# State update laid into the next inverse, and part of the new values' decay on ScalarE, in a gated delta rule recurrence

## The chip, the core and the metric

The kernel runs on one NeuronCore of a Trainium2 chip. The metric is the device time of one execution in microseconds (us). Engines are named as the profile names them: PE is TensorE, DVE is VectorE, ACT is ScalarE, POOL is GpSimd, SP is SyncE, which here only issues DMAs. PE writes its products to PSUM, which has eight banks of 128 x 512 f32; the other engines carry them to SBUF.

## The reference, cut to what matters

Two blocks of a network run one after the other: a mixer with a gated delta rule and a pooling branch, then feed-forward layers, a short convolution and latent attention. Only the gated delta rule is touched. It works on 8 heads in two directions, over 512 tokens (256 of context, then 256 with queries). The reference uses chunks of 64 tokens; the kernel uses chunks of 128, which gives the same values:

```python
a_mat = jnp.where(strict, jnp.einsum('bhncd,bhnsd->bhncs', kb, k) * decay, 0.0)
sol = lax.linalg.triangular_solve(eye + a_mat, rhs, ...)        # rhs = [v*beta, kb*exp(g)]
qk = jnp.einsum('bhncd,bhnsd->bhncs', q, k) * decay
k_tail = k * jnp.exp(g_last[..., None] - g)[..., None]
def step(state, inp):
    v_new = u_i - jnp.einsum('bhcd,bhdv->bhcv', w_i, state)
    o_i = (jnp.einsum('bhcd,bhdv->bhcv', q_i, state)
           + jnp.einsum('bhcs,bhsv->bhcv', qk_i, v_new))
    state = state * jnp.exp(gl_i)[..., None, None] + jnp.einsum('bhcd,bhcv->bhdv', k_i, v_new)
    return state, o_i
```

## The kernel before

**Rounds.** `ROUNDS` (L1167) holds 8 rounds: four chunks (`step_` 0 to 3) times two groups of four heads. A round has two sides, one batch of four heads each: forward (FWD, banks 0 to 2) and backward (BWD, banks 3 to 5). The state that a round reads was made two rounds before, by the same heads. Chunks 0 and 1 are context; in chunks 2 and 3 the outputs of the queries are made as well; chunk 3 makes no state.

**One round.** In the order of PE's program: the inverse of the lower triangular matrix (`inverse`, L1271) by four levels of doubling in 64 x 64 halves, each a left product (L1294) into bank b0+2, an ACT copy (L1468), a right product (L1311) into bank b0+1, a DVE addition (L1621) and a DVE transpose (L1623); the transposes of `a` (L1302) lie in level 1; rounds with queries have the products of keys and queries (L1317) in level 2; then the steps to 64 and 128 tokens (L1326, L1337, L1342, L1351, L1360). After that the keys times the state (L1376, from chunk 1 on), the running sums of the decays for the next round (`sums`, L1248), four parts of the modulation (`some_mods` "state"), the new values (L1386), the Gram matrix of the next round (`gram`, L1256), the outputs (L1398, L1400), two modulation parts ("out"), the new state (L1409), the transposed keys of the next round (`key_rows`, L1268) and six modulation parts ("gram").

**Around PE.** DVE copies the end of the inverse to `xt` (L1643), forms `rhs` (L1651; L1656 in chunk 0), half of the decay argument (L1608, L1609), the new values with their decayed tail (L1662), the masked Gram matrix (L1579), the outputs (L1671, L1674), the state (L1680, L1684) and, last, `first_blocks` (L1582) for both sides, whose result `ac` (L1594) the first left product of the next round waits for. ACT makes the decay (`decay`: four Relu, L1427, and one Exp, L1431), for rounds with queries also a second decay for `pt` (L1441, L1445), and copies. POOL makes masks and products in SBUF: L1522, L1530, L1542, L1548, L1552, L1558.

**Modulation.** In the rounds PE also multiplies 96 parts of 512 KB of another weight matrix (`mod_part`, L577, products at L587), 12 a round, at places fixed by `MOD_SLOTS` (L1181). They come through a ring of six buffers: SP asks for part p once part p-6 is used. The next stage starts on ACT only after the copy of the last group (L613), and the weights of that stage are asked for after the last part.

**Order.** Every engine runs its program in order; all waits between engines are semaphores written out by hand, so an instruction that waits holds all behind it on its engine.

Of the kernel before, what the change touches and what calls it, by code (L numbers as in the profile page):

```python
# [206 lines left out]
def two_block_kernel(nc, stream, modstream, tokens, ctx2, conds, cols_in, consts_in, rope_tab, count_in, out):  # L207
# [47 lines left out]
    for d in (FWD, BWD):  # L255
        for room, names in (("inner", ("ac", "atc")), ("outer", ("xc", "xtc"))):
# [4 lines left out]
            .rearrange("p l (j c) -> p l j c", j=4)  # L261
        W[d]["t1h"] = W[d]["t1"][:, 0:2, :].rearrange("p a b -> p (a b)").rearrange("p (j c) -> p j c", j=4)
# [907 lines left out]
    a_dec, a_pt, a_qd, a_kt, a_at, a_t1, a_vn = (sem(f"a_{n}") for n in ("dec", "pt", "qd", "kt", "at", "t1", "vn"))  # L1170
# [3 lines left out]
    a_pair, a_xt, a_relu, a_ptr = (sem(f"a_{n}") for n in ("pair", "xt", "relu", "ptr"))  # L1174
    xt_clear = sem("xt_clear")
    d_relu = sem("d_relu")
# [4 lines left out]
    MOD_SLOTS = {"state": 4, "out": 2, "gram": 6}  # L1181
# [39 lines left out]
    def packed(b, rows=slice(0, P), width=PAIR):  # L1221

        return bank[b][rows, 0:4 * width].rearrange("p (j c) -> p j c", j=4)
# [5 lines left out]
    def pe_recur(pe):  # L1229
# [14 lines left out]
        def sums(r):  # L1244
            for n, d, t, hs, b0, gc in per_batch(r):
                if r:
                    pe.wait_ge(d_xf, n - 1)
                four(lambda j: nc.tensor.matmul(  # L1248
                    b4(b0)[:, j], gb_tok[:, t, gc][:, j:j + 1].to_broadcast([P, P]), C(Const.INCL[d]),
                    start=True, stop=True), g_cb)  # L1250

        def gram(r):
            for n, d, t, hs, b0, gc in per_batch(r):
                if r:
                    pe.wait_ge(d_rhs, n - 1)
                four(lambda j: nc.tensor.matmul(  # L1256
                    b4(b0 + 1)[:, j], kT[:, hs, tok(t)][:, j], kT[:, hs, tok(t)][:, j],
                    start=True, stop=True), g_gram)

        def key_rows(r):  # L1260
            step_ = ROUNDS[r][0]
            for n, d, t, hs, b0, gc in per_batch(r):
                pe.wait_ge(a_dec, n + 1)
                if step_ >= 2:
                    pe.wait_ge(a_qd, n - X_BATCH0 + 1)
                    pe.wait_ge(a_pt, n - X_BATCH0 + 1)
                if step_ < 3:
                    four(lambda j: nc.tensor.transpose(b4(b0)[:, j], kT[:, hs, tok(t)][:, j],  # L1268
                                                       C(Const.IDENT)), g_kt)

        def inverse(r):  # L1271
# [3 lines left out]
            for li in range(1, 5):  # L1275
                for n, d, t, hs, b0, gc in batches:
                    w = W[d]
                    if li == 1:
                        pe.wait_ge(d_at, n + 1)
                        if r:  # L1280
                            pe.wait_ge(d_vdec, n - 1)
                            if ROUNDS[r - 1][0] < 3:
                                pe.wait_ge(d_state, n - 1)
                            if ROUNDS[r - 1][0] >= 2:
                                pe.wait_ge(d_o, n - 1 - X_BATCH0)
                    elif li == 2:
                        pe.wait_ge(p_at, nth(2, r, 0, d))
                    elif li == 4:
                        pe.wait_ge(p_at, nth(2, r, 1, d))
                    pe.wait_ge(d_xm, nth(5, r, li - 1, d))  # L1290
                    at_li = w["ac"] if li == 1 else w["atl"][:, li % 2]
                    for j in range(4):
                        for i in range(2):
                            last = nc.tensor.matmul(packed(b0 + 2, half(i))[:, j], at_li[half(i), j], w["xc"][half(i), j],  # L1294
                                                    start=True, stop=True)
                    last.then_inc(g_p1, 1)
                if li == 1:
                    for n, d, t, hs, b0, gc in batches:
                        pe.wait_ge(d_a, n + 1)
                        if step_ < 3:  # L1300
                            pe.wait_ge(a_kt, n + 1)
                        four(lambda j: nc.tensor.transpose(b4(b0)[:, j], W[d]["a"][:, j], C(Const.IDENT)), g_at)  # L1302
                for n, d, t, hs, b0, gc in batches:
                    w = W[d]
                    pe.wait_ge(a_t1, nth(6, r, li - 1, d))
                    pe.wait_ge(d_xt, nth(5, r, li - 1, d))
                    if li == 1:
                        pe.wait_ge(d_gm, n + 1)
                    for j in range(4):
                        for i in range(2):  # L1310
                            last = nc.tensor.matmul(packed(b0 + 1, half(i))[:, j], w["xtc"][half(i), j],  # L1311
                                                    w["t1h"][half(i), j], start=True, stop=True)
                    last.then_inc(g_p2, 1)
                if li == 2 and with_x:
# [54 lines left out]
        for r, (step_, hg) in enumerate(ROUNDS):  # L1369
# [8 lines left out]
            if r + 1 < len(ROUNDS):  # L1378
                sums(r + 1)
# [8 lines left out]
            if r + 1 < len(ROUNDS):  # L1388
                gram(r + 1)
# [1205 lines left out]
```

## Time and profile before

| | us |
|---|---|
| median of 3 runs (2462.14 to 2470.65) | 2464.55 |
| the profiled execution | 2467.92 |
| its span in the profile | 2466.1 |
| recurrence, first sums to the first product of the next stage | 323.10 to 658.18 |
| PE busy in the span | 2328.3 (94%) |
| DVE, ACT, POOL busy | 966.4, 791.2, 1025.9 |
| mean granted clock of PE | 0.958 |

Below, a round is counted from the first record of L1360 of the round before to its own first L1360; the inner stretches of the first group of rows are cut there. The rows that the prediction rests on stand in a section below.

### The profile page before, as it was taken

How to read it: one execution, taken by the hardware profiler on the slowest of the kernel's cores; microseconds unless marked ns; L12 is line 12 of the kernel's file. 1: busy time of each engine (PE TensorE's matmuls, PEld its weight loads, DVE VectorE, ACT ScalarE, POOL GpSimd, SP SyncE). 2: the span in 40 equal slices, each digit the busy share in tenths (PEclk: the TensorE clock that was granted, in tenths of full speed). 3: DMA queues.
4: the chain of work that ended last, by engine and by line, in shares of the span. 5: the costliest groups of instructions: out<-in, count | busy, mean ns of one | idle time of the engine just before them, and what ended most of it. 6: DMA issues, size and time to landing. Idle time of an engine off the chain costs nothing.

```text
span 2466.1 us, 36821 instructions
## 1 busy us (share of the span) xinstructions
PE 2328.3 (94%) x14268; PEld 1852.7 (75%) x14268; DVE 966.4 (39%) x1631; ACT 791.2 (32%) x1247; POOL 1025.9 (42%) x473
## 2 busy tenths in 40 slices
PE   6998788898889999999999999999999999898999
PEld 2787667676667888887887888887888887547999
DVE  4459656656363121124455122124112114755212
ACT  2443423334223222223223222223222222424444
POOL 1445612233252444443443444443444443304888
PEclk8999878999898999999999999999999999989999
DMA  6334414525561433332532533332433332202656
GB/s 244 94 104 128 162 54 154 206 105 183 181 232 63 162 94 94 94 94 86 171 94 77 171 94 95 94 94 77 160 96 95 94 94 77 74 0 81 189 179 184
DMA packets 82682, 297.38 MB, mean 121 GB/s; under 512 B 9072, under 2 KB 11504, under 8 KB 82288
## 3 DMA queue, kind: packets, MB, share of 16 engines
q1 hardware_dynamic: 82400, 295.03, 37.1%
q8 instruction: 107, 1.75, 0.3%
q10 hardware_dynamic: 144, 0.34, 0.0%
q14 instruction: 31, 0.25, 0.0%
HBM read 294.28 MB, written 1.05 MB: 120 GB/s over the span
## 4 chain that ended last, share of the span: by engine, by line
PE 77%; issue 11%; DVE 6%; POOL 4%; ACT 1%; DMA 1%; POOLq 0%; SPq 0%; DVEq 0%; ACTq 0%
PE bank L547 21%; PE bank L544 21%; PE bank L543 21%; POOL w_lo L519 4%; PE bank L587 2%; PE bank L1294 1%; PE bank L1311 1%; PE bank L1248 1%; PE bank L918 1%; DVE gdn_inner L1588 1%; PE bank L2147 1%; DVE nt L751 1%; PE bank L2148 1%; PE bank L1376 1%; PE bank L1256 1%
## 5 line engine op out<-in xcount | busy, mean ns | idle before, releaser
L519 POOL TENSOR_TENSOR w_lo<-w_raw,w_hi 128x1024 fp32r<-128x1024 f32 x383 | 934.7, 2444 | 1181.2 <-ACT w_hi L771 1180.9
L543 PE MATMUL bank<-n_hi,w_lo 128*128 128x512 f32 (+1 forms) x2216 | 793.3, 358 | 30.9 <-POOL w_lo L519 16.3
L547 PE MATMUL bank<-n_lo,w_hi 128*128 128x512 f32 (+1 forms) x2216 | 792.1, 357 | 0.6 <-DVE n_lo L695 0.3
L544 PE MATMUL bank<-n_hi,w_hi 128*128 128x512 f32 (+1 forms) x2216 | 791.3, 357 | 0.0
L771 ACT CAST w_hi<-w_raw 128x1024 fp32r<-128x1024 f32 x383 | 401.1, 1049 | 776.1 <-PE bank L547 766.3
L543 PEld LDWEIGHTS bank<-n_hi,w_lo 128*128 128x128 f32 x2216 | 423.4, 191 | 116.3 <-issue 44.6
L544 PEld LDWEIGHTS bank<-n_hi,w_hi 128*128 128x128 f32 x2216 | 423.6, 191 | 64.5
L547 PEld LDWEIGHTS bank<-n_lo,w_hi 128*128 128x128 f32 x2216 | 422.6, 191 | 64.6 <-DVE n_lo L695 2.5
L1955 DVE TENSOR_TENSOR prod<-silu,bank 128x512 f32<-128x512 f32 (+1 forms) x88 | 54.6, 622 | 728.9 <-PE bank L547 721.4
L544 PE MATMUL bank<-g_hi,w_hi 128*128 128x512 f32 (+1 forms) x768 | 284.1, 370 | 0.0
L547 PE MATMUL bank<-g_lo,w_hi 128*128 128x512 f32 (+1 forms) x768 | 284.1, 370 | 0.0
L543 PE MATMUL bank<-g_hi,w_lo 128*128 128x512 f32 (+1 forms) x768 | 282.3, 368 | 1.1 <-DVE g_lo L1946 1.1
L1917 DVE SCALAR_TENSOR_TENSOR h<-bank,gates,h 128x256 f32<-128x256 f32 x136 | 60.7, 481 | 301.2 <-PE bank L547 301.1
L543 PEld LDWEIGHTS bank<-g_hi,w_lo 128*128 128x128 f32 x768 | 144.4, 188 | 29.1 <-DVE g_lo L1946 1.5
L544 PEld LDWEIGHTS bank<-g_hi,w_hi 128*128 128x128 f32 x768 | 144.3, 188 | 27.4
L547 PEld LDWEIGHTS bank<-g_lo,w_hi 128*128 128x128 f32 x768 | 144.1, 188 | 26.1
L1903 ACT ACTIVATE silu<-bank 128x512 f32<-128x512 f32 (+1 forms) x88 | 47.7, 544 | 286.1 <-PE bank L547 286.0
L1035 DVE SCALAR_TENSOR_TENSOR conv<-bank,cols,conv 128x508 f32<-128x508 f32 (+3 forms) x96 | 63.0, 659 | 60.7 <-ACT conv L975 58.1
L1946 DVE TENSOR_TENSOR g_lo<-prod,g_hi 128x512 fp32r<-128x512 f32 (+1 forms) x88 | 82.8, 943 | 1.8 <-ACT g_hi L1893 1.5
L751 DVE TENSOR_TENSOR nt<-h 128x512 f32<-128x512 f32 (+1 forms) x77 | 78.6, 1021 | 2.6
L587 PE MATMUL bank<-mod_raw,cond 128*32 128x512 f32 x256 | 54.9, 694 | 22.0 <-DMA mod_raw<-in_modstream 18.3
L756 DVE TENSOR_TENSOR sq_acc<-sq_acc,nt 128x512 f32<-128x512 f32 (+1 forms) x66 | 62.0, 939 | 2.3
(317 smaller groups left out, 2036.3 us busy)
## 6 DMA issues: line engine op xcount, KB each, us to landing
w_raw<-in_stream SPq DMA_DIRECT2D x383, 512.0 KB, 3.6
mod_raw<-in_modstream SPq DMA_DIRECT2D x64, 512.0 KB, 4.6
late<-in_modstream SPq DMA_DIRECT2D x56, 512.0 KB, 4.7
w_raw<-in_modstream SPq DMA_DIRECT2D x48, 512.0 KB, 6.2
h<-in_tokens SPq DMA_DIRECT2D x1, 2048.0 KB, 10.8
consts<-in_consts SPq DMA_DIRECT2D x1, 1152.0 KB, 9.9
h<-in_ctx SPq DMA_DIRECT2D x1, 1024.0 KB, 8.7
out<-h SPq DMA_DIRECT2D x8, 128.0 KB, 3.6
```

The costliest lines, as they stand in the source:

```text
L519: nc.gpsimd.tensor_tensor(w_lo[:, slot, :], w_raw[:, slot, :], w_hi[:, slot, :].bitcast(F32), ALU.subtract).then_inc(w_lo_ready, 1)
L543: nc.tensor.matmul(out_ap, wl, hi, start=start, stop=False)
L544: nc.tensor.matmul(out_ap, wh, hi, start=False, stop=False)
L547: return nc.tensor.matmul(out_ap, wh, lo, start=False, stop=stop)
L587: last = nc.tensor.matmul(bank[MOD_BANK][32 * j:32 * j + 32, :], cond[:, which, k, :], room[:, jj * 512:(jj + 1) * 512], start=(k == 0), s ...
L751: square = nc.vector.tensor_tensor(nt[:, k % 2, s_], h[:, k, s_], h[:, k, s_], ALU.mult)
L756: ins = nc.vector.tensor_tensor(sq_acc[:, s_], sq_acc[:, s_], nt[:, k % 2, s_], ALU.add)
L771: nc.scalar.copy(w_hi[:, c % RING, :], w_raw[:, c % RING, :]).then_inc(w_hi_ready, 1)
L1035: ins = nc.vector.scalar_tensor_tensor(acc[:, :, to], src[:, :, of], col(Cols.CONV + ci * CONV + j), acc[:, :, to], ALU.mult, ALU.add)
L1917: last = nc.vector.scalar_tensor_tensor(h[:, d, s_], bank[g % BANKS][:, s_], gates[:, gate, d, c:c + 1], h[:, d, s_], ALU.mult, ALU.add)
L1946: nc.vector.tensor_tensor(g_lo[:, f, 0:w], prod[:, f % 2, 0:w], g_hi[:, f, 0:w].bitcast(F32), ALU.subtract).then_inc(hid_lo, 1)
L1955: nc.vector.tensor_tensor(prod[:, f % 2, 0:w], silu[:, f % 2, 0:w], bank[g % BANKS][:, 0:w], ALU.mult).then_inc(groups_read, 2)
```

## The change

It reorders the recurrence and moves some of its work between engines; the same 96 modulation parts and the same products are made.

- The new state of round r-1 (`new_state`) is made inside the inverse of round r: after the first left product of the forward side if round r-1 had no queries, after level 1 if it was of chunk 2. DVE's `state_sum` follows behind levels 1 to 3.
- The transposed keys (`key_rows`) are made in their own round, behind level 1, instead of one round ahead; the transposes of `a` go from level 1 to behind level 2, the products of keys and queries from level 2 to level 3, the keys times the state from behind the inverse to between left and right product of level 4. `rhs` is formed right behind level 4.
- After the inverse PE runs, side by side, Gram matrix, sums, new values of FWD, then the same of BWD.
- Left products write to the upper half of bank b0+1, not to bank b0+2.
- In the rounds without queries (chunks 0 and 1) the decayed tail of the new values is made by ACT (four Identity with a scale, semaphore `a_vdec`), not by DVE. In chunk 3 it is not made at all.
- ACT makes the decay argument of both sides, with Abs in the place of Relu; DVE's L1608 and L1609 are gone. `pt` is now masked `dec` (by POOL); ACT's second decay (L1441, L1445) is gone.
- DVE's `first_blocks` no longer holds the product L1600; it is `whole`, behind the additions of level 1. Its waits at the joint: Gram matrix of both sides before `first_blocks` of FWD.
- POOL: the mask of level 2 (`at2`) is a product of its own right behind `atc`; `atl` holds levels 3 and 4; beta masks are made into `a` one round ahead.
- Modulation parts: "first" 2 (in level 1), "half" 3 (behind L1326), "last" 3 (behind L1351), "key" 4 (end of the round).

```diff
-    MOD_SLOTS = {"state": 4, "out": 2, "gram": 6}
+    MOD_SLOTS = {"first": 2, "half": 3, "last": 3, "key": 4}
...
+        def gram(r, side):
+            n, d, t, hs, b0, gc = per_batch(r)[side]
+            if r:
+                pe.wait_ge(a_t1, nth(6, r - 1, 5, d))
+                pe.wait_ge(d_half, n - 1)
...
+        def new_state(r):
+            for n, d, t, hs, b0, gc in per_batch(r):
+                if ROUNDS[r][0] < 2:
+                    pe.wait_ge(a_vdec, n + 1)
+                else:
+                    pe.wait_ge(d_vdec, n - X_BATCH0 + 1)
+                    pe.wait_ge(d_o, n - X_BATCH0 + 1)
+                four(lambda j: nc.tensor.matmul(b4(b0 + 2)[:, j], W[d]["ktok"][:, j], W[d]["rhs"][:, j],
+                                                start=True, stop=True), g_st)
...
+            late_state = r and ROUNDS[r - 1][0] == 2
+            left(r, 1, FWD)
+            if r and ROUNDS[r - 1][0] < 2:
+                new_state(r - 1)
+            right(r, 1, FWD)
+            some_mods(r, "first")
+            left(r, 1, BWD)
+            right(r, 1, BWD)
+            if late_state:
+                new_state(r - 1)
+            if step_ < 3:
+                key_rows(r)
+            for d in (FWD, BWD):
+                left(r, 2, d)
+            for d in (FWD, BWD):
+                right(r, 2, d)
...
+            for d in (FWD, BWD):
+                left(r, 4, d)
+            for d in (FWD, BWD):
+                keys_state(r, d)
+            for d in (FWD, BWD):
+                right(r, 4, d)
...
                 last.then_inc(g_p1, 1)
+            some_mods(r, "half")
...
                 last.then_inc(g_p1, 1)
+            some_mods(r, "last")
...
             inverse(r)
...
+            for d in (FWD, BWD):
+                if r + 1 < len(ROUNDS):
+                    gram(r + 1, d)
+                    sums(r + 1, d)
+                new_values(r, d)
+            if step_ >= 2:
...
+            some_mods(r, "key")
...
+            for n, d, t, hs, b0, gc in batches:
+                if r + 1 < len(ROUNDS):
+                    decay(r + 1, d)
+                if not with_x:
+                    act.wait_ge(g_vn, n + 1)
+                    for j in range(4):
+                        last = nc.scalar.activation(W[d]["rhs"][:, j], b4(b0 + 2)[:, j], ACT.Identity,
+                                                    scale=e_tail[:, t, gc.start + j:gc.start + j + 1])
+                    last.then_inc(a_vdec, 1)
...
+            more = r + 1 < len(ROUNDS)
+            if more:
+                masked_gram(r + 1, FWD)
+            values_decay(r, FWD)
+            if more:
+                masked_gram(r + 1, BWD)
+                first_blocks(r + 1, FWD)
+            values_decay(r, BWD)
+            if more:
+                first_blocks(r + 1, BWD)
+            turned_groups(r, "key")
```

## Rows read from the trace of the kernel before

**Rows 1.** Windows: stretch, length, busy PE PEld DVE ACT POOL (records), clock, DMA, GB/s.
```profile
323.10:351.86 28.76, 22.18 (x401) 20.15 (x401) 16.89 (x38) 9.55 (x25) 4.09 (x4) 0.80 0.01 2
351.86:388.98 37.12, 33.73 (x497) 25.78 (x497) 23.11 (x46) 11.45 (x31) 8.30 (x8) 0.87 0.47 171
388.98:426.29 37.31, 34.39 (x500) 25.90 (x500) 23.30 (x48) 12.00 (x32) 8.30 (x8) 0.86 0.48 171
426.29:463.91 37.62, 34.02 (x516) 26.75 (x516) 23.69 (x60) 12.01 (x32) 8.12 (x8) 0.91 0.47 169
463.91:504.26 40.35, 36.40 (x529) 28.77 (x529) 24.63 (x60) 16.21 (x44) 13.00 (x12) 0.92 0.44 158
504.26:548.71 44.45, 39.92 (x565) 32.57 (x565) 26.16 (x64) 17.02 (x45) 13.09 (x12) 0.92 0.40 143
548.71:591.99 43.28, 38.90 (x557) 31.68 (x557) 26.23 (x64) 16.53 (x44) 13.05 (x12) 0.92 0.43 148
591.99:631.27 39.28, 35.28 (x540) 27.12 (x540) 23.92 (x56) 16.43 (x44) 13.09 (x12) 0.96 0.46 162
631.27:658.18 26.91, 20.11 (x132) 12.63 (x133) 9.36 (x22) 5.82 (x12) 4.97 (x4) 0.75 0.49 173
```
**Rows 2.** The chain that ended last, over one joint: start, length, what.
```profile
390.60 3.78 PE bank L1248 x16
394.38 2.49 PE bank L587 x16
396.87 1.98 PE bank L1386 x16
398.86 1.79 PE bank L1256 x16
400.64 1.00 PE bank L587 x8
401.64 2.00 PE bank L1409 x16
...
408.47 1.41 DVE gdn_inner L1588
...
411.51 0.68 PE bank L1294 x16
...
417.49 0.43 DVE gdn_outer L1621
...
422.49 0.43 DVE gdn_outer L1621
```
**Rows 3.** Timeline, PE: start, length, engine, line, operation, tiles, forms, records.
```profile
592.98 2.05 PE L1376 MATMUL bank<-state,kT 128*128 128x128 f32 x16
366.12 1.04 PE L1268 MATMUL bank<-consts,kT 128*128 128x128 f32 x8
```
**Rows 4.** Timeline, DVE, ACT and POOL, same columns; idle time before in brackets.
```profile
392.71 1.14 ACT L1427 ACTIVATE gdn_dec<-bank,neg_cum 128x128 f32<-128x128 f32 x4 [1.84 <-PE bank L1248]
393.89 0.63 ACT L1431 ACTIVATE gdn_dec<-gdn_dec 128x512 f32<-128x512 f32 x1
408.21 1.37 POOL L1542 TENSOR_TENSOR gdn_dec<-gdn_inner,consts 128x512 f32<-128x512 f32 x1 [3.30 <-DVE gdn_a L1600]
440.30 2.16 DVE L1684 SCALAR_TENSOR_TENSOR state<-state,e_tot,bank 128x128 f32<-128x128 f32 x8 [1.32 <-PE bank L1409]
```
**Rows 5.** Two stretches behind the inverse, columns as in rows 1.
```profile
388.98:395.00 6.02, 6.00 (x36) 5.10 (x40) 3.47 (x5) 3.62 (x10) 2.22 (x2) 0.50 0.01 3
591.99:595.00 3.01, 3.01 (x34) 2.94 (x35) 1.60 (x5) 1.85 (x5) 1.80 (x2) 1.00 0.00 0
```
**Rows 6.** Timeline: ACT changing its table, and PE around the end of the recurrence.
```profile
301.71 1.28 ACT L1014 ACT_TABLE_LOAD   x1
645.43 1.07 PE L587 MATMUL bank<-w_raw,cond 128*32 128x512 f32 x8
651.25 1.57 PE L587 MATMUL bank<-w_raw,cond 128*32 128x512 f32 x4 [0.19 <-DMA w_raw<-in_modstream]
```

More of the change, by code:

```diff
@@ new lines, in left @@
+        def left(r, li, side):
+            n, d, t, hs, b0, gc = per_batch(r)[side]
+            w = W[d]
+            if li == 1:
+                pe.wait_ge(d_at, n + 1)
+                pe.wait_ge(d_gm, n + 1)
+            elif li == 2:
+                pe.wait_ge(p_at, nth(2, r, 0, d))
+            elif li == 3:
+                pe.wait_ge(p_at, nth(2, r, 1, d))
+            pe.wait_ge(d_xm, nth(5, r, li - 1, d))
+            at_li = w["ac"] if li == 1 else w["at2"] if li == 2 else w["atl"][:, li - 3]
+            for j in range(4):
+                for i in range(2):
+                    last = nc.tensor.matmul(upper(b0 + 1, half(i))[:, j], at_li[half(i), j], w["xc"][half(i), j],
+                                            start=True, stop=True)
+            last.then_inc(g_p1, 1)
@@ new lines, in right @@
+        def right(r, li, side):
+            n, d, t, hs, b0, gc = per_batch(r)[side]
+            w = W[d]
+            pe.wait_ge(a_t1, nth(6, r, li - 1, d))
+            pe.wait_ge(d_xt, nth(5, r, li - 1, d))
+            for j in range(4):
+                for i in range(2):
+                    last = nc.tensor.matmul(packed(b0 + 1, half(i))[:, j], w["xtc"][half(i), j],
+                                            w["t1h"][half(i), j], start=True, stop=True)
+            last.then_inc(g_p2, 1)
@@ L1274, in inverse @@
             with_x = step_ >= 2
-            for li in range(1, 5):
-                for n, d, t, hs, b0, gc in batches:
[L1277 to L1314, printed above, removed]
-                    for n, d, t, hs, b0, gc in batches:
-                        pe.wait_ge(a_at, n + 1)
-                        four(lambda j: nc.tensor.matmul(b4(b0)[:, j], kT[:, hs, tok(t)][:, j],
-                                                        qT[:, hs, tok(t)][:, j], start=True, stop=True), g_qk)
@@ L1483, in act_recur @@
                 act.wait_ge(g_p1, nth(6, r, 5, d))
-                nc.scalar.copy(W[d]["t1h"][hi], packed(b0 + 2, hi)).then_inc(a_t1, 1)
+                nc.scalar.copy(W[d]["t1h"][hi], upper(b0 + 1, hi)).then_inc(a_t1, 1)
+            mods_copied(r, "last")
             for n, d, t, hs, b0, gc in batches:
@@ L1616, in dve_recur @@
             with_x = step_ >= 2
-            for li in range(1, 5):
+            late = r and ROUNDS[r - 1][0] == 2
+            if r and ROUNDS[r - 1][0] >= 2:
+                outputs(r - 1)
+            for d in (FWD, BWD):
+                add_level(r, 1, d)
+                whole(r, d)
+            turned_groups(r, "first")
+            if r and not late:
+                state_sum(r - 1, FWD)
+            for d in (FWD, BWD):
+                add_level(r, 2, d)
+            if r:
+                state_sum(r - 1, FWD if late else BWD)
```

450 lines of the change are left out of this document (225 added, 225 removed).

## The prediction

> **What bounds the kernel now.** I read first the windows over the recurrence [rows 1]. It is 335.1 us of the 2466.1 us span, and only it and the hand-over behind it are touched. PE is busy for about nine tenths of each round (33.7 of 37.1 us, 39.9 of 44.5 us), so PE's program, in order, is the bound; two things make its round long. First, the clock: in rounds 1 to 7 it is 0.86 to 0.96. A stretch that is at half clock for half its length has a mean of 0.75 and could be a quarter shorter, so the time that a full clock could save is at most (1 - clock) times the length: 4.8, 5.2, 3.4, 3.2, 3.6, 3.5 and 1.6 us, 25.3 us in all. Second, the joint between rounds. The chain of waits shows it [rows 2]: behind the inverse PE runs sums, modulation, new values, Gram matrix, modulation and state one after the other (390.60 to 403.6); then the chain leaves PE and goes through DVE's two `first_blocks`, until the left product at 411.51. In those 8 us PE has only modulation and one side's left product. The clock view of the stretches says when the clock falls: behind the run of 32 x 32 and 64 x 64 products it was 0.50 for 6 us in one round and stayed 1.00 in another [rows 5].
>
> **The sum, part by part.** I lay round 2 (37.31 us before, 388.98 to 426.29) out anew from S, the first L1360, at full clock. Durations: eight products of 128 x 128 take 1.79 to 2.05 us (0.9 a side) [rows 2, 3]; a transposition of both sides 1.0 [rows 3]; two modulation parts 1.0 [rows 2]; one level of doubling 2.5 (417.49 to 422.49 are two) [rows 2].
>
> 1. Joint. L1360 1.1 (estimate: its share at full clock), then Gram, sums, new values, F and B: 6 x 0.9 = 5.4, at 6.5. "key" four parts 2.0, at 8.5. Who is late next? ACT's decay of F waits for the sums of F (2.9): 1.14 + 0.63 [rows 4] gives 4.8; the decayed tail of F four small activations, about the 1.14 of L1427, 6.0; decay of B 7.8; tail of B 9.0. DVE: Gram B 5.5, `first_blocks` F without L1600 about 3.0, `ac` at 8.1, B `ac` at 11.5. Both come before PE wants them, within half a microsecond for F; so they are covered, and each microsecond by which ACT or DVE is later costs one.
> 2. Level 1. Left F 0.6, new state 2.0 (its wait for ACT's tail of B, 9.0, is met at 9.1; queued behind it are right F and all of the inverse), right F 0.6, two parts 1.0, left B 0.6, gap for the ACT copy 0.5, right B 0.6: at 14.4. Keys 1.0: 15.4.
> 3. Levels 2 and 3 with the transposes of `a`: 2.5 + 1.0 + 2.5, at 21.4. DVE has two additions with transposes, `whole` 0.65 and 1.1 of L1684 a level, which fits in 2.5 + 1.0. A POOL product of SBUF beside L1684 did not lengthen it (2.16 for eight [rows 4]).
> 4. Level 4 with the keys times the state: 2.5 + 2.0 less the 0.5 gap that these fill, at 25.4.
> 5. Last steps: from the addition at 422.49 to L1360 at 426.29 are 3.8, that is 3.2 from the end of the right product of B. Now 3 + 3 parts lie in them, 3.0, and nothing hides these: 31.6.
>
> So 31.6 against 37.3. PE's work is the same; what goes is the stretch of `first_blocks` in which it had little to do, and half clock behind the inverse. DVE's L1608, L1609 and L1662 and ACT's L1441 and L1445 go too; the walk above has them left out already, and they are worth nothing beyond that. No modulation part should wait for its data: a part of "key" reuses a buffer that was free with "half" or "last", at least 6 us before.
>
> A collision: the chain has a `first_blocks` product of 1.41 us instead of 0.42, beside a POOL product of 1.37 [rows 2, 4]. `at2` on POOL starts as DVE does L1592 and L1594. Bounds a side: 0, or the whole of `at2`, 0.7 (estimate: half the elements of L1542 and its 1.37). I take 0 on the path, since `ac` of F has 0.4 to spare and `ac` of B 2, and keep 0.3 a round, 2 us, for the range. The Trainium skill (SBUF — State Buffer, "SBUF: two separate sides") says that a DVE operation with two SBUF inputs and a GpSimd operation exclude each other for the whole instruction. By that rule every round would pay the upper bound, and the sum would be 2 us less gain; the trace agrees with it in the one pair of rows.
>
> The other rounds, by the same walk: round 1 (no keys times state) 29.9; round 3 31.6; round 4 (keys times queries, 1.5 net of a hidden gap) 33.2. Rounds 5 to 7 have the outputs in the joint. The new values of B are decayed by DVE behind `first_blocks` F (9.6), ACT's copy follows (10.3), so the outputs of B run 10.4 to 12.2, "key" ends at 14.1 and all is 5.6 later than in round 2; with the new state behind level 1: round 5 39.5, round 6 (no keys) 38.5, round 7 (no state either) 36.7.
>
> | | before [rows 1] | new | gain |
> |---|---|---|---|
> | 1 | 37.1 | 29.9 | 7.2 |
> | 2, 3 | 37.3, 37.6 | 31.6 each | 5.7, 6.0 |
> | 4 | 40.4 | 33.2 | 7.2 |
> | 5 | 44.5 | 39.5 | 5.0 |
> | 6 | 43.3 | 38.5 | 4.8 |
> | 7 | 39.3 | 36.7 | 2.6 |
>
> That is 38.5. The first stretch (28.8) gets the keys and eight modulation parts before its L1360, and its `first_blocks` B is 1 us shorter; its clock is 0.80, so I add 2.8: -2.8. The last stretch: today outputs end 14.2 behind S (645.43), the last part is used only at 652.8, since two buffers came free late (PE waits for DMA at 651.25 [rows 6]), and the next stage starts 5.4 later (658.18). Anew: xt and new values F at 2.9, B at 3.8, outputs to 7.5, with latencies 8.1; four parts, data long there, 2.0; then the same 5.4 and 0.7 for DVE's squares beside POOL's products: 16.2 against 26.9, 10.7 gained. Sum: 38.5 - 2.8 + 10.7 = 46.4 us.
>
> The clock: the walk took it as full. The new order puts 512-column products into the run behind which it fell, and takes away PE's idle stretch, but a PE that is now the bound pays every half-clock microsecond. Bounds: 0, and the 25.3 us of today. I take a quarter, 6.5, nearer to the stretch that stayed at 1.00 [rows 5]. So 2467.9 (the profiled execution) - 46.4 + 6.5 = 2428.0; the median of the runs lies 3.4 below that execution: **2424.5**.
>
> **The rivals.**
> - *The clock falls as it did.* The joint's gain comes, the clock's doesn't: 46.4 - 25.3 = 21, 2443.5. For it: the long middle of the inverse is unchanged small products. Against: they ran at 1.00 before, and the fall came behind the smallest.
> - *ACT is late at the new wait.* If Abs and Exp need different tables, each batch of decays pays 2 x 1.28 [rows 6], 5.1 a round before the tail of B; `new_state` waits 4.8 in rounds 1 to 4, the outputs of B 2.6 in 5 to 7: 27 us back, 2451.5. Against: Relu and Exp have stood side by side with no load between them [rows 4]. The Trainium skill (ScalarE: Activation LUTs, "Table sets: the hidden batching unit") says that abs is in every set; by it there is no load, and by its 2.7 us a switch the loss would be twice mine. No row here shows Abs.
> - *The time was covered anyway*: the joint's waits come back as DVE's chain (`first_blocks` 3 us later than in the walk in every round, from new latencies). 7 rounds x 3 to 5 us off a gain of 40 leave 5 to 19; at the small end 2459.5, no change.
> - *Slower: PE stays at half clock.* The work of a round is now one chain of short products with ACT and DVE between; if the granted clock is that of the last stretch, 0.75 [rows 1], a round of 40 us pays 10, seven pay 70: 46.4 - 70 = -23.6, 2488. It decides from a mean clock under 0.83 in the rounds (46.4 over 280 us); the lowest of them today is 0.86, so it must get worse than in any round shown.
>
> **How the numbers follow.** Forecast 0.62; clock as before 0.17; ACT late 0.07; covered anyway 0.07; slower 0.07. The forecast's own range is 2412 (clock full, all of the 46 and some) to 2437. To leave out no more than 2 in 10 the range goes up to the clock rival: 2411 to 2446. A measurement of this kernel can tell about 0.3%, 7.4 us, from no change. Faster by more than that are the first three and 0.02 of the fourth, 0.88; the rest of the fourth is no change, 0.05; slower 0.07.
>
> **What would show it.** Rounds of 30 to 33 us between first L1360s in 1 to 4 and 37 to 40 in 5 to 7; granted clock 0.95 or more in them; PE's idle before the first left product under 1 us; no DMA wait at L587; no ACT table load in the rounds; L1588's twin for B at 0.42. Wrong if PE waits for `a_vdec` before the new state, if `ac` of F comes more than 1 us behind the "key" parts, if outputs of B start over 11 us behind S, or if the last stretch stays over 20 us.

## The result

| | before | after |
|---|---|---|
| median of 4 runs, us | 2464.91 (2462.14 to 2470.65) | 2430.30 (2425.90 to 2433.95) |
| profiled execution, its span | 2467.92, 2466.1 | 2428.83, 2427.0 |
| ratio of the times, 95% interval | | 0.9856, 0.9831 to 0.9881 |
| first stretch: first sums to first L1360 (before), L1421 (after) | 28.76 | 31.35 |
| rounds 1 to 7, sum | 279.4 | 249.1 |
| last stretch: from there to the first product of the next stage | 26.91 | 15.59 |

The times are 1.4% shorter, where 2424.5 in a range of 2411 to 2446 was forecast. L1421 is the line that was L1360. To be set against the rows of before [rows 1], the windows of the kernel after, cut at its first L1421 of each inverse (stretch, length, busy PE PEld DVE ACT POOL with records, granted clock, DMA share, GB/s):

```profile
323.10:355.82 32.72, 27.02 (x434) 19.64 (x433) 17.33 (x40) 11.87 (x33) 8.16 (x8) 0.86 0.21 68
355.82:387.77 31.95, 30.04 (x503) 22.10 (x501) 18.52 (x42) 15.38 (x45) 8.16 (x8) 1.00 0.59 215
387.77:420.08 32.31, 31.08 (x516) 23.71 (x513) 20.17 (x50) 12.82 (x38) 8.16 (x8) 1.00 0.52 181
420.08:452.96 32.88, 31.74 (x518) 24.04 (x517) 21.04 (x56) 15.96 (x46) 8.16 (x8) 1.00 0.56 194
452.96:487.78 34.82, 33.58 (x535) 25.99 (x533) 22.62 (x58) 15.68 (x46) 13.26 (x12) 1.00 0.50 184
487.78:529.61 41.83, 37.63 (x567) 29.51 (x565) 24.95 (x60) 15.60 (x41) 13.27 (x12) 1.00 0.46 165
529.61:568.81 39.20, 35.83 (x556) 28.41 (x553) 25.20 (x62) 12.03 (x32) 13.27 (x12) 1.00 0.40 145
568.81:604.91 36.10, 34.35 (x542) 26.78 (x541) 21.69 (x52) 15.17 (x40) 11.28 (x10) 1.00 0.51 181
604.91:620.50 15.59, 9.13 (x86) 7.18 (x85) 7.61 (x12) 4.42 (x9) 5.40 (x4) 0.95 0.53 198
```

Two things are to be seen. The clock column is 1.00 in all seven rounds (before 0.86 to 0.96). And a round of 32.31 us has 31.08 of PE busy, so 1.2 us of idle where there were 2.9. Over rounds 1 to 7, with the same products, PE is busy for 234.3 us instead of 252.6 and idle for 14.8 instead of 26.8: of the 30.3 us by which the rounds are shorter, 18.3 are busy time, the same products at a higher clock, and 12.0 are waiting that is gone. In this execution the first sums begin at 324.47, 1.37 later than before, so the first stretch is 31.35 long. From first sums to the next stage the recurrence takes 296.0 instead of 335.1, 39.1 less; the span is 39.1 shorter. Outside the recurrence nothing was gained on balance: 1.4 us more ahead of it, 1.4 less behind (1806.5 against 1807.9).

What PE still waits for in rounds 1 to 7 (line, who ends the wait, us in all, times, longest). L1309 is a right product, L1447 the outputs, L1385 the first products of the step to 64, L588 a modulation part:

```profile
PE bank L1309 <- ACT gdn_t L1479: 4.7, 10, 0.5
PE bank L1447 <- DVE gdn_rhs L1688: 3.5, 2, 1.8
PE bank L1385 <- DVE gdn_outer L1654: 2.4, 7, 0.3
PE bank L588 <- ACT mod_row L614: 1.6, 2, 0.8
```

The 15.1 us that PE waited for DVE's `ac` before (L1594) have no line any more. The joint of round 2, in which this was won; S, its first L1421, is at 387.77. The columns are start, length, engine, line; `ac` is written by L1639, and L1582 is POOL's `at2`:

```profile
392.61 0.69 DVE L1624 SCALAR_TENSOR_TENSOR gdn_a<-bank,gdn_a 128x512 f32<-128x512 f32 x1 [1.99 <-PE bank L1261]
393.21 0.84 DVE L1633 TENSOR_TENSOR gdn_inner<-gdn_a,gdn_dec 64x256 f32<-64x256 f32 x2
...
395.22 0.95 DVE L1639 TENSOR_TENSOR gdn_inner<-gdn_inner,consts 128x256 f32<-128x256 f32 x1
...
398.44 0.95 DVE L1639 TENSOR_TENSOR gdn_inner<-gdn_inner,consts 128x256 f32<-128x256 f32 x1
...
395.08 0.82 POOL L1582 TENSOR_TENSOR gdn_t<-gdn_inner,consts 128x256 f32<-128x256 f32 x1 [17.89 <-DVE gdn_inner L1636]
...
395.18 1.12 ACT L1536 ACTIVATE gdn_rhs<-bank,e_tail 128x128 f32<-128x128 f32 x4
```

`ac` F is ready at 396.17, 8.4 behind S, as the four parts of "key" end; ACT's tail of B at 396.30 (8.5); `ac` B at 399.39 (11.6), a microsecond before its left product (400.43).

### The profile page after: what moved, and what is told of

It is laid out like the page before. It is cut to its first block, busy times and chain, and to the rows that moved or that the text cites. A ratio compares the mean times of both kernels' runs of the same rounds, so it can differ in the third digit from the quotient of the medians.

```text
span 2427.0 us, 36815 instructions
## 1 busy us (share of the span) xinstructions
PE 2302.1 (95%) x14268; PEld 1826.4 (75%) x14268; DVE 948.4 (39%) x1603; ACT 793.1 (33%) x1271; POOL 1027.2 (42%) x473
## 4 chain that ended last, share of the span: by engine, by line
issue 52%; PE 23%; POOL 20%; DVE 4%; ACT 1%; POOLq 1%; DVEq 0%; ACTq 0%
POOL w_lo L520 20%; PE bank L544 3%; PE bank L545 3%; PE bank L548 3%; PE bank L588 2%; PE bank L1298 1%; PE bank L1309 1%; PE bank L919 1%; PE bank L2218 1%; PE bank L1261 1%; PE bank L2219 1%; PE bank L2259 1%; PE bank L1281 0%; PE bank L1252 0%; PE bank L2236 0%
## 5 line engine op out<-in xcount | busy, mean ns | idle before, releaser
L1582 POOL TENSOR_TENSOR gdn_t<-gdn_inner,consts 128x256 f32<-128x256 f32 x16 | 13.1, 817 | 174.6 <-DVE gdn_inner L1636 174.6
L588 PE MATMUL bank<-mod_raw,cond 128*32 128x512 f32 x256 | 62.2, 685 | 18.8 <-DMA mod_raw<-in_modstream 18.8
```

The lines of the kernel that those rows point to most:

```text
L588: last = nc.tensor.matmul(bank[MOD_BANK][32 * j:32 * j + 32, :], cond[:, which, k, :], room[:, jj * 512:(jj + 1) * 512], start=(k == 0), s ...
```

## The experiments

Where the order is the same and the clock full, round lengths repeat to 0.1 us from one profiled execution to another (rounds 1 to 4 of after, a_vdecb), so each run is read by its rounds, and the total only confirms. Each run has one profile; where the clock falls in a run is known from that one alone. "Falls" counts the stretches of 1 us windows with the clock under 0.95, behind an inverse (eight of them) and elsewhere in rounds 1 to 7.

| run | median us | ratio to before | rounds 1 to 7 | last stretch | falls behind the inverse / elsewhere |
|---|---|---|---|---|---|
| before | 2464.9 | | 279.4 | 26.9 | 7 / 6 |
| after | 2430.3 | 0.9856 | 249.1 | 15.6 | 0 / 0 |
| b_slots | 2462.8 | 0.9994 (0.9984 to 1.0003) | 281.9 | 19.0 | 0 / 7 |
| a_slots | 2483.1 | 1.0081 (1.0064 to 1.0098) | 295.3 | 20.3 | 6 / 0 |
| a_mid | 2454.8 | 0.9953 (0.9937 to 0.9968) | 271.0 | 17.6 | 8 / 0 |
| a_mid2 | 2443.9 | 0.9916 (0.9898 to 0.9935) | 255.9 | 18.2 | 5 / 0 |
| a_joint | 2445.9 | 0.9926 (0.9910 to 0.9943) | 265.2 | 15.6 | 0 / 2 |
| a_state | 2429.1 | 0.9862 (0.9846 to 0.9879) | 251.1 | 15.6 | 0 / 0 |
| a_dvestate | 2451.4 | 0.9939 (0.9918 to 0.9959) | 274.9 | 15.6 | 0 / 4 |
| a_both | 2454.9 | 0.9952 (0.9936 to 0.9967) | 276.7 | 15.6 | 0 / 5 |
| a_vdec | 2426.9 | 0.9843 (0.9816 to 0.9869) | 249.3 | 15.6 | 0 / 0 |
| a_vdecb | 2423.6 | 0.9832 (0.9805 to 0.9860) | 245.1 | 15.6 | 0 / 0 |
| a_at2 | 2429.9 | 0.9852 (0.9823 to 0.9882) | 247.5 | 15.6 | 0 / 0 |
| a_best | 2420.4 | 0.9813 (0.9800 to 0.9827) | 244.8 | 11.8 | 0 / 0 |

The ratio is to the kernel before as it ran beside each run. The code cuts below are shortened; what stands in them as a comment tells what is left out.

My theory was that the gain has two parts, a shorter joint (`ac` comes in time) and the clock (by where the modulation parts stand). The rivals: all is clock; or all is order.

The falls elsewhere go with waits of PE in the joint. All 24 of them (in five of the kernels) begin during, or within 2.3 us behind, a wait of 1.5 to 3.6 us, 20 times the wait for `ac`. Such a wait did not always bring one: a_joint has four waits for `ac` of up to 1.9 us in rounds 1 to 4 and no fall there.

**b_slots: the parts moved, in the kernel before.**

```diff
-    MOD_SLOTS = {"state": 4, "out": 2, "gram": 6}
+    MOD_SLOTS = {"half": 3, "last": 3, "state": 2, "gram": 4}
```

> The kernel before with the modulation parts alone moved: three behind the 32 x 32 products, three behind the last left products of 64 x 64, two in "state", four in "gram", none in "out". My theory: two separate gains. The clock follows the place of the wide products, so it is 0.97 or more in rounds 1 to 7 (before 0.86 to 0.96); but the joint keeps its order, and with six parts fewer in it PE idles about 3 us more a round before the first left product. A round with no queries is 36 to 37.5 us (before 37.1 to 37.6), the last stretch some 5 us shorter: total 2452 to 2462. Rival (all is clock): rounds 1 to 4 fall to 32 to 35 us as in the changed kernel, total about 2435. Rival (place of the parts does nothing to the clock): clock stays 0.86 to 0.96, total 2465 or more.

Measured 2462.8, no change, and 0.8 us above what I expected. The clock of the rounds is 0.92 to 0.96, not the 0.97 that I expected: the falls behind the inverse are gone, but seven others stand in the joints. PE's wait for `ac` over rounds 1 to 7 in the kernel before, then round 2 of this one as a window and the same wait:

```profile
PE bank L1294 <- DVE gdn_inner L1594: 15.1, 6, 3.5
```
```profile
394.68:431.16 36.48, 30.97 (x504) 23.46 (x500) 23.27 (x48) 11.36 (x31) 8.35 (x8) 0.95 0.47 165
```
```profile
PE bank L1294 <- DVE gdn_inner L1596: 25.2, 12, 3.6
```

The clock rose from 0.86 to 0.95 and PE's busy time fell by 3.4 us [rows 1], but the round is only 0.8 shorter. PE waits for `ac` 10 us longer in the seven rounds: the joint ran at DVE's pace, and what PE saved it idled. "All is clock" falls here, since moving the parts alone gave nothing. In all, the rounds are 2.5 longer and the first stretch, which gets the six parts of "half" and "last", 4.4; the last stretch is 7.9 shorter. So most of the 11.3 us that the changed kernel gains in the last stretch can be had by the place of the parts alone.

**a_slots, a_mid, a_mid2: the parts moved, in the kernel after.**

```diff
-    MOD_SLOTS = {"first": 2, "half": 3, "last": 3, "key": 4}
+    MOD_SLOTS = {"first": 5, "half": 0, "last": 0, "key": 7}        # a_slots
+    MOD_SLOTS = {"first": 2, "mid": 6, "key": 4}                    # a_mid: "mid" ahead of left product 3
```

> The changed kernel with its modulation parts put together around the joint: five in "first", seven in "key", none in "half" and "last". My theory: the clock falls behind the smallest products as in the kernel before, mean 0.88 to 0.96 in rounds 1 to 7, which costs 12 to 25 us in the rounds, and the last stretch grows by 2 to 6 us for parts that come late: total 2444 to 2458. Rival (the clock is held up by the absence of PE's idle stretch, not by the parts' place): clock 1.00, rounds as in the changed kernel within 0.5 us, total 2430 to 2436.

Measured 2483.1, beyond both. Twelve parts close together ("key", then "first") need their data faster than they come: over the recurrence PE waited 14.2 us for DMA (12.3 for `w_raw`, 1.9 for `mod_raw`), and 8.1 for the half copies L1738 that stand behind `rhs` in DVE's program. So this run can't price the clock, which fell behind six of eight inverses. It led to a_mid, which spreads the data as before.

> The changed kernel with the six modulation parts of "half" and "last" put together into the middle of the inverse, between the transposes of `a` and level 3, so that the data come as evenly as before and the joint keeps its four parts. My theory: parts beside the smallest products do two things, they keep the clock up behind the inverse and they hide `rhs` and ACT's last copies. So the clock falls to one half for 4 us or more behind the inverse in most rounds (2 us or more each), PE waits 1.4 us for the half copies and up to 1 us for copies of ACT: rounds 1 to 7 longer by 3 to 5 us each, total 2451 to 2464. Rival (the clock fell only because PE idled in the joint): clock 1.00 in rounds 1 to 7, the waits alone remain, 1.4 to 2.5 us a round, total 2440 to 2448.

Measured 2454.8, in the range expected: rounds 21.9 longer in all (2.3 to 4.7 each, where I said 3 to 5), and the clock falls behind every inverse. Round 3's beginning, in windows of 1 us:

```profile
422.00:423.00 1.00, 0.96 (x63) 0.85 (x56) 1.00 (x5) 0.65 (x3) 0.00 (x0) 1.00 0.09 37
423.00:424.00 1.00, 0.19 (x13) 0.08 (x6) 1.00 (x5) 0.64 (x3) 0.00 (x0) 1.00 0.08 20
424.00:425.00 1.00, 0.46 (x9) 0.46 (x11) 0.75 (x3) 0.00 (x0) 0.00 (x0) 1.00 0.00 0
425.00:426.00 1.00, 0.87 (x15) 0.72 (x13) 0.00 (x0) 0.72 (x3) 0.00 (x0) 0.70 0.00 0
426.00:427.00 1.00, 1.00 (x16) 1.00 (x14) 0.18 (x1) 0.96 (x4) 0.00 (x0) 0.50 0.02 8
```

and its wait for the half copies over the rounds:

```profile
PE bank L1411 <- DVE gdn_outer L1737: 8.1, 6, 1.4
```

PE waits 1.35 us for the half copies, until 424.54, and about 0.9 us later, at 425.4, is at half clock. So the idle, not the lack of wide products, could be the cause; a_mid2 takes that wait away:

```diff
             for n, d, t, hs, b0, gc in batches:
+                src, dst = first_pair(d)
+                dve.wait_ge(g_p2, nth(5, r, 4, d))         # and the half copy itself
+            for n, d, t, hs, b0, gc in batches:
                 w = W[d]
                 dve.wait_ge(p_rhs, n + 1)
...
-                src, dst = first_pair(d)
-                dve.wait_ge(g_p2, nth(5, r, 4, d))         # and the half copy itself
```

> As the run with the six parts in the middle of the inverse, and DVE makes the two half copies ahead of `rhs`, so that PE's 1.4 us of idle before the last left products goes. It tells apart what lets the clock fall behind the inverse. Theory 1 (idle of PE): with the wait gone the clock stays 1.00 in rounds 2 to 7, which are shorter by 1.4 for the wait and by 1.5 to 3 for the clock: total 2430 to 2438. Theory 2 (small products without wide ones beside them, idle or not): the falls behind the inverse stay in every round at 0.57 for 4 to 8 us, rounds are shorter by 1.4 at most, total 2445 to 2449. I think the first the likelier, since in the trace of that run the fall begins 1 us behind the idle stretch.

Measured 2443.9, between the two. The rounds are 15.1 us shorter, 8.1 of it the wait; the falls went from eight to five. My likelier theory was too simple. In two rounds whose last microseconds are alike, the clock fell once and once not:

```profile
425.00:426.00 1.00, 0.75 (x40) 0.67 (x40) 0.67 (x3) 0.43 (x2) 0.00 (x0) 1.00 0.17 66
```

That window stands 1.7 us ahead of S of round 3 (427.66), behind which the clock was 0.50; the one in the same place of round 4 had 0.76 busy and kept 1.00. The lack of wide products is enough in some rounds. That idle ahead of the smallest products makes the fall surer is a hint, eight falls against five with one profile of each. With three parts at each of the two places (after, b_slots) it fell behind none of sixteen. Why it falls in one of two like rounds stays open.

**a_joint: the products of the joint in sequence.**

```diff
             for d in (FWD, BWD):
-                if r + 1 < len(ROUNDS):
+                if more:
+                    sums(r + 1, d)
+            for d in (FWD, BWD):
+                new_values(r, d)
+            for d in (FWD, BWD):
+                if more:
                     gram(r + 1, d)
-                    sums(r + 1, d)
-                new_values(r, d)
```

> The changed kernel with the joint in sequence on PE as before: sums of both sides, new values of both, Gram matrix of both. Everything else stays. My theory: the masked Gram matrix of the forward side starts 3.6 us later but the decay is there earlier, so its `ac` comes 1 to 2.5 us later and the left product waits: rounds 1 to 4 longer by 1 to 2.5 us each, rounds 5 to 7 by under 0.5 (the outputs cover it), total 2435 to 2440. Rival (DVE's path is covered anyway, the joint's order is worth nothing): rounds within 0.3 us, total 2428 to 2433.

Measured 2445.9, more than expected. Rounds 1 to 4 are 2.1, 2.1, 1.5 and 2.1 longer, within what I worked out (1 to 2.5). In round 2 `ac` of F comes 10.5 behind S instead of 8.4, and the left product starts at 10.53 instead of 8.46, after 1.9 of waiting: what `ac` is late, the round is longer. Rounds 5 and 6 are 4.0 longer each, where I said under 0.5. I had taken the outputs as cover, but they wait themselves: for the decayed values (L1692), which stand in DVE's program behind Gram matrices that now come later, four times and 7.2 us instead of twice and 3.5. The clock falls once in each of the two rounds (mean 0.96). The waits for these two over rounds 1 to 7:

```profile
PE bank L1451 <- DVE gdn_rhs L1692: 7.2, 4, 2.4
PE bank L1298 <- DVE gdn_inner L1643: 6.8, 4, 1.9
```

**a_state and a_dvestate: the state back in its own round,** first PE's product alone, then DVE's sums as well.

```diff
-            if r and ROUNDS[r - 1][0] < 2:
-                new_state(r - 1)
...
-            if late_state:
-                new_state(r - 1)
...
             some_mods(r, "key")
+            if step_ < 3:
+                new_state(r)                       # a_dvestate: ahead of "key"
...
+            for d in (FWD, BWD):
+                state_sum(r, d)                    # a_dvestate alone, DVE, ahead of both first_blocks;
+                                                   # ahead of it the outputs of chunk 2
```

> The changed kernel with the new state not laid over the next inverse but made at the end of its own round, behind "key"; DVE's part of it stays where it is. My theory: the overlay itself is worth little, since the new state now covers DVE's `first_blocks` as well there; what is lost is the cover of ACT's copy between left and right product, 0.5 us in rounds 1 to 4, and 0 to 0.5 in rounds 5 and 6: total 2431 to 2435. Rival (the overlay carries the gain): every one of rounds 1 to 6 longer by 1.5 to 2 us, total 2440 to 2444.

Measured 2429.1, below the 2431 to 2435 expected: a total of four runs doesn't resolve 2 us. The rounds do, and are as expected: 1 to 6 are longer by 0.4, 0.4, 0.5, 0.4, 0.2 and 0.2, 2.0 in all. What it loses is cover of ACT's copy (PE waits 6.6 for it, not 4.7).

> The changed kernel with the whole state part taken out of the next inverse, PE's and DVE's: PE makes the new state in its own round ahead of "key", and DVE makes its sums ahead of `first_blocks` (and the outputs of chunk 2 ahead of them), as before. My theory: what counts is DVE's order. ACT's tail of B is there 8.5 us behind S, the new state of F starts then at the latest, both end near 10.5, DVE's sums at 12.5, `ac` of F 3 us later at about 15.5, where the left product now starts at 8.5 and "key" can hide 2: rounds 1 to 4 longer by 3.5 to 6 us, rounds 5 and 6 by 3 to 6, with PE waiting for `ac`; clock below 1.00 again behind these waits: total 2450 to 2466. Rival (the overlay is worth as little here as when PE's product alone was moved, and the gain is the order of the joint's products): total 2429 to 2437.

Measured 2451.4: rounds 1 to 6 longer by 4.0, 6.3, 3.8, 5.4, 4.5 and 1.9, where I said 3.5 to 6 for 1 to 4 and 3 to 6 for 5 and 6. The joint of round 2 (S = 390.65):

```profile
395.49 0.69 DVE L1621 SCALAR_TENSOR_TENSOR gdn_a<-bank,gdn_a 128x512 f32<-128x512 f32 x1 [1.99 <-PE bank L1261]
398.10 0.69 DVE L1673 TENSOR_SCALAR state<-bank 128x512 f32<-128x512 f32 x1 [1.92 <-PE bank L1281]
400.45 0.69 DVE L1673 TENSOR_SCALAR state<-bank 128x512 f32<-128x512 f32 x1 [1.65 <-PE bank L1281]
401.06 0.84 DVE L1630 TENSOR_TENSOR gdn_inner<-gdn_a,gdn_dec 64x256 f32<-64x256 f32 x2
403.06 0.94 DVE L1636 TENSOR_TENSOR gdn_inner<-gdn_inner,consts 128x256 f32<-128x256 f32 x1
...
404.06 0.68 PE L1298 MATMUL bank<-gdn_outer,gdn_inner 64*64 64x64 f32 x16 [1.80 <-DVE gdn_inner L1636]
```

DVE is idle 1.9 and 1.7 us here with the masked Gram matrix long made: it waits for a state product that ACT's tail releases, and `first_blocks` stands behind that. `ac` comes at 404.0, 13.4 behind S instead of 8.4. So of "state laid over the inverse" PE's half alone is worth 2 us of rounds (a_state), and both halves together 26. The 24 between them I put down to DVE's order, but they aren't DVE's alone: PE's product stands ahead of "key" here, where it waits 4.8 us for ACT's tail, and the clock falls in four rounds. Of the 25.9 us 15.6 are more idle of PE, 12.6 of them the wait for `ac`; the rest is busy time at a lower clock.

**a_both: the two undone together** (the edits of a_joint and a_dvestate).

> The changed kernel with two parts undone together: the joint in sequence on PE (sums, new values, Gram matrix), alone worth 15.5 us, and the state part of PE and DVE back in its own round ahead of `first_blocks`, alone worth 21 us. My theory: both lie on the same chain into `first_blocks`, which starts when the later of Gram matrix (7) and state (12) is done, so undoing both costs little more than undoing the second: total 2451 to 2457. Rival (two separate gains that add up): 2464 to 2470, which is the kernel before.

Measured 2454.9: rounds 27.6 longer, where the two alone are 16.1 and 25.9. They lie on one chain into `first_blocks`. With it the rounds are back to within 2.7 us of the kernel before. That kernel took 2465.9 beside it, 11.0 more; by the windows 10.0 of them are 2.7 of rounds and 11.3 of last stretch, less 4.0 by which its first stretch is shorter. So the parts of the change that a_both leaves in (the modulation parts' places, decay on ACT, L1600 out of `first_blocks`, transposes and keys moved) are together worth 2.7 us of rounds once these two are undone; of the last three none was undone alone.

**a_vdec: the tail of the values of chunks 0 and 1 on DVE again.**

```diff
-            if ROUNDS[r][0] == 2:
+            if ROUNDS[r][0] < 3:
                 dve.wait_ge(g_vn, n + 1)
                 tt(W[d]["rhs"][:], b4(b0 + 2), bc(e_tail[:, t, gc]), ALU.mult).then_inc(d_vdec, 1)
```

> The changed kernel with the decayed tail of the new values of chunks 0 and 1 made by DVE again (0.67 us a side, forward between the two masked Gram matrices, backward between the two `first_blocks`), not by ACT. My theory: DVE has the time; the tail of B is there at 9.6, the new state of B starts at 10.0, `ac` of B goes from 11.5 to 12.2 where its left product starts at 12.7: rounds 1 to 4 within 0.3 us, total 2428 to 2433. Rival (DVE is the bound in the joint, so its 1.3 us come out in full): rounds 1 to 4 longer by 0.7 to 1.4 each, total 2433 to 2436.

Measured 2426.9, 1.1 below what I expected; rounds 1 to 4 differ by 0.0, 0.0, 0.0 and 0.25. This half of the change is worth nothing either way, though DVE is 1.3 us busier in a round (21.47 against 20.17 in round 2).

**a_vdecb: DVE's decayed values of B ahead of `first_blocks` of F.**

```diff
                 masked_gram(r + 1, BWD)
-                first_blocks(r + 1, FWD)
             values_decay(r, BWD)
+            if more:
+                first_blocks(r + 1, FWD)
```

> The changed kernel, and DVE makes the decayed values of B ahead of `first_blocks` of F. It changes only the joints behind the two rounds of chunk 2, in which PE waited twice 1.8 us for that product before the outputs of B. My theory: both waits go, `ac` of F comes 0.7 later and is still 4 us early: rounds 5 and 6 shorter by 1.5 to 1.8 us each, total 2426 to 2428. Rival (another wait, for ACT's copy of the values or for POOL's `qdec`, takes its place): rounds within 0.5 us, total 2430.

Measured 2423.6, better than the 2426 to 2428 expected; rounds 5 and 6 are 39.82 and 37.19, 2.0 shorter each, and L1447 has no wait left.

**a_at2: POOL's product out of DVE's way.**

```diff
-                pool.wait_ge(d_atc, n + 1)
+                pool.wait_ge(d_at, n + 1)
                 tt(w["at2"], ...)
```

> The changed kernel, and POOL's product `at2` waits for DVE's `ac` instead of running beside it. My theory: the 0.5 us by which DVE's product grew (0.95 instead of 0.43) goes, but nobody waits for it but by a tenth: rounds within 0.3 us, total 2428 to 2433. Rival (by the rule that each lock between DVE and POOL is paid): each of rounds 1 to 7 shorter by 0.5 to 1, total 2423 to 2427. If the product still takes 0.95 us, the growth isn't the collision.

The product in round 2 (length in ns: shortest, median, longest; then the first and last start):

```profile
L1639 DVE TENSOR_TENSOR gdn_inner<-gdn_inner,consts x2: 414/416/417, 395.3 to 398.4; 128x256 f32<-128x256 f32 x2
```

Measured 2429.9. The product is back from 951 ns to 416. The rounds are shorter by 0.2, 0.2, 0, 0.1, 0.5, 0.5 and 0: 1.5 us in all, two of them more than the 0.3 that I expected. The collision is real, its price is the part that someone waits for. In rounds 1, 2 and 4 that is the first left product, which starts 0.06 behind `ac` in round 2 of the kernel after; in rounds 5 and 6 the outputs of B, which wait for DVE's work behind it (2.5 us in all, not 3.5).

**a_best: these two, and the hand-over mended.** In the last stretch of the kernel after, PE waits 5.5 us for `y_lo`, behind DVE's squares:

```profile
615.37 4.39 DVE L1859 TENSOR_TENSOR qT<-o_sum 128x512 f32<-128x512 f32 x4
619.67 2.48 DVE L1862 TENSOR_TENSOR n_lo<-y_pool,n_hi 128x512 fp32r<-128x512 f32 x4
...
612.60 5.40 POOL L1833 TENSOR_TENSOR z_dn<-z_dn,o_sum 128x512 f32<-128x512 f32 x4 [18.77 <-DVE o_sum L1667]
```

```diff
         outputs(len(ROUNDS) - 1)
+        dve.wait_ge(d_o, 8)
+        # squares 0 and 1
         dve_mod_bias(dve, RECUR_LAST)
...
-        # squares 0 to 3, then y_lo 0 to 3
+        # y_lo 0, squares 2 and 3, y_lo 1 to 3
```

> The changed kernel with the two small finds and a mended hand-over: decayed values of B ahead of `first_blocks` (alone -4.0 us in rounds 5 and 6), `at2` behind `ac` (-0.15 in three of the rounds without outputs), and in the last stretch two of DVE's four squares ahead of its modulation bias and the first `y_lo` ahead of the other two squares, since PE waits 5.5 us there for `y_lo` behind 4.4 us of squares. My theory: PE starts the next stage 3 to 4 us earlier, and the total is 2420 to 2424. Rival (the wait moves to PE's third block, which needs the squares): the last stretch gains 3 us and the next one loses them, total 2425 to 2427.

Its last stretch, the first `y_lo` in the timeline, and what PE waits for there:

```profile
600.16:612.00 11.84, 9.13 (x86) 7.18 (x85) 6.23 (x10) 4.43 (x9) 4.14 (x3) 1.00 0.40 132
```
```profile
610.62 1.24 DVE L1864 TENSOR_TENSOR n_lo<-y_pool,n_hi 128x512 fp32r<-128x512 f32 x1
```
```profile
PE bank L544 <- DVE n_lo L1864: 1.7, 1, 1.7
```

Measured 2420.4, ratio 0.9813 (0.9800 to 0.9827): faster than both kernels. The last stretch is 3.8 shorter. The 1806.6 us behind it are what they were (1806.5); that alone says little, since in the other runs with the same code there they are 1804.0 to 1809.3. But PE's waits in the 88 us behind the hand-over are the same too (6.1 for L757, 3.4 against 3.6 for DMA, 1.7 for L681), so the wait did not move to the third block.

## Why the prediction was right, step by step

Right in sign and within 0.25% in size. The mechanism is borne out; that the number came so near is in part luck, since terms that were 8.1 and 6.5 us off had opposite signs. Of the 5.8 us between 2424.5 and 2430.3 only 0.8 lies in the profiled executions (2428.0 forecast, 2428.83 measured). The rest comes from taking the median 3.4 below the profiled execution: after, it was 1.5 above.

- **Joint.** `ac` F forecast at 8.1, measured 8.4; `ac` B 11.5 and 11.6; "key" 8.5 and 8.4; ACT's tail of B 9.0 and 8.5. That they are covered, with nothing to spare for F, and that each microsecond more costs one, a_joint shows from the other side: `ac` of F 2.1 later, rounds 1, 2 and 4 2.1 longer. The stretch ahead of the left product before held one thing more than the text names, the transposed keys (L1268, 1.0 us at 403.45).
- **Levels and state.** Level 4 was to end at 25.4; in round 2 the last right product ends at 25.6. `a_kt`, `p_at` and the rest were never late.
- **Last steps, mis-sized.** Six parts at 0.5 were 3.0; three parts take 1.84 where two take 1.0 and four 2.0, so 3.7. The other steps took 3.0 instead of 3.2, and level 4 ended 0.2 later: together the 0.7 by which round 2 is longer than forecast.
- **Left out.** The end of a group of the modulation: one step of L599 (0.58) and a wait for the copy of `mod_row` (0.8) in some rounds. With the parts' 0.7 these are all of round 1's 2.05 (31.95 against 29.9) and most of round 5's 2.3. The products of keys and queries were priced at 1.5, net of a gap that they hide; they took 2.0, since there was no gap left in level 3 to hide: in round 2, without them, its right products start at 407.63, as the left ones end. Rounds 1 to 7 sum to 249.1, forecast 241.0.
- **Clock, mis-sized the other way.** I kept 6.5 us for it; none was spent in the rounds. The 8.1 and the 6.5 nearly cancel, which is luck. The reason I gave, wide products in the run behind which it fell, is borne out (b_slots has no fall behind the inverse, a_mid one behind each). The second part of the reason, PE's idle stretch in the joint, my text named and did not price: where it came back (b_slots, a_dvestate, a_both), the clock fell there.
- **Outputs.** B was to start at 10.4 with DVE's decay at 9.6: 10.07 after a wait of 1.8. The wait was in my numbers but not recognised as one that a swap removes (a_vdecb, 4.0 us in two rounds). It was also laid on round 7, whose joint is that of chunk 3 and makes no decayed tail: "key" starts there at 10.0, forecast 12.2. That is why round 7 is 0.6 shorter than forecast while all others are longer.
- **The collision.** Kept at 0 to 2 us; 1.5 by a_at2. Each of DVE's products beside POOL's 0.82 us takes 0.95 instead of 0.42. The Trainium skill (SBUF — State Buffer, "SBUF: two separate sides") says that of a DVE operation with two SBUF inputs and a GpSimd operation that reads SBUF, the one waits for the other's whole instruction; the trace agrees to about 0.15 us: POOL's product ends at 395.90, and DVE's 0.27 behind it. The prediction gives 2 us for the case that every round pays, but that is its own 0.3 a round; its upper bound of 0.7 a side is 4.9 us over seven rounds for one side alone. As a price per round it would have been too high.
- **First stretch** -2.8 forecast, -2.6. **Last stretch** 16.2 forecast, 15.6: the last outputs are read at 611.83, 6.9 behind S (forecast: made by 7.5), no part waits for DMA, and then PE waits for DVE, as before.
- **ACT late** did not happen: no table load stands in rounds 1 to 7, and four Abs take 1.14 to 1.16 us where four Relu took 1.14 [rows 4]. The Trainium skill (ScalarE: Activation LUTs, "Table sets: the hidden batching unit") says that abs is in every set; the trace agrees.
- **The other rivals.** *The clock falls as it did* comes nearest in a_mid, which has this joint and a fall behind every inverse: 2454.8, of which 8.1 us are another wait. It costs 17.7 us by (1 - clock) times the length, against 25.3 before. So the joint's gain without the clock's is still faster than the kernel before. "Covered anyway" came in none of the chain's members but ACT's tail (a_vdec) and PE's half of the overlay (a_state). *Half clock throughout*: the rounds ran at 1.00.

## What to carry to other kernels

Ask of a joint whose engine it is before counting what another engine saves: in b_slots the 3.4 us that PE saved in round 2 came back as waiting for DVE, and PE's state product alone, moved into the next inverse, was worth 2 us, where the whole move with DVE's sums was worth 26. Spread independent wide products to where the main chain has the smallest ones: here they hid copies, had their data in time, and the clock stayed up. Price a collision by who waits for the slowed operation, and look behind the last step for an engine that does what nobody needs yet ahead of what the next stage waits for.

## What was not expected of the hardware

- Two rounds with the same work in their last microseconds (busy 0.75 and 0.76, then 1.00, 0.83) ended one at half clock for 3.4 us, one at full clock (a_mid2). In the kernel with the parts back beside the smallest products it fell in none of eight.
- Three modulation parts of 512 columns between small products took 1.84 us, two 1.0, four 2.0. The trace of the kernel after shows why (start, length, line): the products of two parts, which write four different quarters of a bank (L588), start within 0.02 us of each other and run side by side; those of the third run two by two and take 0.86 us, nearly as long as a pair of parts. So an odd part costs almost what two cost, and 4 and 2 parts at the two places would be about 0.7 us a round shorter (an estimate, 2.0 + 1.0 against 2 x 1.84; no run has it).

```profile
414.66 0.62 PE L588 MATMUL bank<-mod_raw,cond 128*32 128x512 f32 x2
414.68 0.62 PE L588 MATMUL bank<-w_raw,cond 128*32 128x512 f32 x2
415.12 0.60 PE L588 MATMUL bank<-mod_raw,cond 128*32 128x512 f32 x2
415.13 1.44 PE L588 MATMUL bank<-w_raw,cond 128*32 128x512 f32 x6
416.50 0.34 PE L1397 MATMUL bank<-gdn_t,gdn_outer 32*32 32x32 f32 x5
```

- POOL's products of two operands in SBUF slow DVE's (0.95 instead of 0.42) and are slowed: four of them took 5.40 us beside four of DVE's squares (4.39), and 6.84 in a_best, where more of DVE's work lay beside them.
